# Opening of a two-layer encoder summed on TensorE, the recurrence's output transposed one unit later, and one weight's low part moved

## The reference

```python
mods = (jax.nn.silu(c) @ ada_w[i] + ada_b[i]).reshape(bsz, 9, D_MODEL)
h = _modulate(x, mods, 0)                       # x * (1 + scale) + shift
y = _swiglu(h, ffn_w_in[i, 0], ffn_w_out[i, 0])
x = _layer_norm(ALPHA * x + 0.5 * mods[:, 2, None, :] * y, ...)
...
# mixer of layer 1, per head of 128 channels, chunks of 64 tokens, both directions
state = dcy[..., None] * state + einsum('bhsd,bhsv->bhdv', kd, vc)
o = o_f + o_b
o = o * lax.rsqrt(mean(square(o)) + LN_EPS)
o = o * norm_g * silu(gate);  return o @ w_out
```

## Time and profile before

| | us |
|---|---|
| median of 3 runs | 2140.7 (2138.68 to 2141.26) |
| profiled execution, its own time | 2141.63 |
| span of the profiled execution | 2139.9 |
| TensorE matmuls busy | 2097.4 (98%) |
| VectorE busy | 1199.3 (56%) |
| ScalarE busy | 784.7 (37%) |
| GpSimd busy | 246.0 (11%) |

### The profile page before, as it was taken

How to read it: one execution, slowest core, us unless ns; L and a number is a source line. 1 busy time by engine, 2 the same in 40 slices (tenths; PEclk the granted TensorE clock), 3 DMA queues, 4 the chain that set the end, 5 groups by cost and what they waited for, 6 DMA issues and landing times.

```text
span 2139.9 us, 30931 instructions
## 1 busy us (share of the span) xinstructions
PE 2097.4 (98%) x10775; PEld 1720.5 (80%) x10775; DVE 1199.3 (56%) x1878; ACT 784.7 (37%) x1142; POOL 246.0 (11%) x238
## 2 busy tenths in 40 slices
PE   7999999999999999999999999999999999999997
PEld 5788888878888888888888888877878788888886
DVE  6766665655557666654535533467676555333344
ACT  4321222455434222222532222376666545322222
POOL 0000000432113000001300000151121131000002
PEclk9999999999999999999999999999999999999999
DMA  9766752332325657643335632332222123323322
GB/s 319 216 184 196 219 174 72 88 109 80 106 70 186 188 176 226 195 125 101 89 98 164 179 98 76 101 102 77 70 77 69 40 70 99 91 85 113 95 73 84
DMA packets 405669, 266.34 MB, mean 124 GB/s; under 512 B 9416, under 2 KB 366184, under 8 KB 405608
## 3 DMA queue, kind: packets, MB, share of 16 engines
q1 hardware_dynamic: 405608, 265.57, 41.5%
HBM read 263.37 MB, written 2.19 MB: 124 GB/s over the span
## 4 chain that ended last, share of the span: by engine, by line
PE 92%; ACT 3%; DVE 3%; issue 1%; POOL 1%; DMA 0%; SPq 0%; ACTq 0%; POOLq 0%; DVEq 0%
PE ps L1483 26%; PE ps L1485 26%; PE ps L1484 26%; PE ps L1498 1%; PE ps L1499 1%; PE ps L1523 1%; PE ps L1761 1%; PE ps L1504 1%; PE ps L1682 1%; PE ps L1708 1%; PE ps L1529 1%; PE ps L1693 1%; DVE w_lo L837 1%; PE ps L1779 1%; PE ps L1515 1%
## 5 line engine op out<-in xcount | busy, mean ns | idle before, releaser
L837 DVE TENSOR_TENSOR w_lo<-raw,w_hi 128x1024 fp32r<-128x1024 f32 (+2 forms) x384 | 429.1, 1119 | 699.4 <-ACT w_hi L601 699.2
L601 ACT ACTIVATE w_hi<-raw 128x1024 fp32r<-128x1024 f32 (+2 forms) x384 | 371.6, 969 | 1104.9 <-PE ps L1485 1067.2
L1483 PE MATMUL ps<-h_hi,w_hi 128*128 128x512 f32 x1744 | 686.8, 394 | 3.6 <-DVE g L846 2.2
L1485 PE MATMUL ps<-h_hi,w_lo 128*128 128x512 f32 x1744 | 679.4, 390 | 0.0
L1484 PE MATMUL ps<-h_lo,w_hi 128*128 128x512 f32 x1744 | 678.9, 389 | 0.0
L1483 PEld LDWEIGHTS ps<-h_hi,w_hi 128*128 128x128 f32 x1744 | 327.4, 188 | 79.0 <-issue 8.3
L1485 PEld LDWEIGHTS ps<-h_hi,w_lo 128*128 128x128 f32 x1744 | 327.4, 188 | 68.9
L1484 PEld LDWEIGHTS ps<-h_lo,w_hi 128*128 128x128 f32 x1744 | 327.6, 188 | 65.9
L1483 PE MATMUL ps<-g_hi,w_hi 128*128 128x512 f32 x704 | 276.0, 392 | 0.0
L1485 PE MATMUL ps<-g_hi,w_lo 128*128 128x512 f32 x704 | 274.1, 389 | 0.0
L1484 PE MATMUL ps<-g_lo,w_hi 128*128 128x512 f32 x704 | 274.0, 389 | 0.0
(11 more groups left out here) (252 smaller groups left out, 1943.6 us busy)
## 6 DMA issues: line engine op xcount, KB each, us to landing
raw<-in_ffn_w_in_dram SPq DMA_DIRECT2D x176, 512.0 KB, 3.7
ada_raw<-in_ada_w_dram SPq DMA_DIRECT2D x128, 512.0 KB, 4.3
raw<-in_ffn_w_out_dram SPq DMA_DIRECT2D x64, 384.0 KB, 3.4
raw<-in_ffn_w_out_dram SPq DMA_DIRECT2D x64, 320.0 KB, 3.1
raw<-in_hgrn_w_in_dram SPq DMA_DIRECT2D x40, 512.0 KB, 3.7
raw<-in_na_w_qkv_dram SPq DMA_DIRECT2D x24, 512.0 KB, 3.7
boot<-in_ada_w_dram SPq DMA_DIRECT2D x8, 512.0 KB, 6.8
boot<-in_ada_w_dram SPq DMA_DIRECT2D x16, 256.0 KB, 6.1
```

Source lines behind the costliest of these rows:

```text
L601: nc.scalar.activation(w_hi[s][:, 0:ph.kt, :], raw[s][:, 0:ph.kt, :], ACT.Copy).then_inc(S.w_hi_done, 1)
L837: nc.vector.tensor_tensor(w_lo[s][:, 0:ph.kt, :], raw[s][:, 0:ph.kt, :], w_hi[s][:, 0:ph.kt, :].bitcast(F32), ALU.subtract).then_inc(S.w_l ...
L1483: nc.tensor.matmul(ps[:, bank, :], w_hi[s][:, k, :], a, start=start and k == 0, stop=False)
L1485: ins = nc.tensor.matmul(ps[:, bank, :], w_lo[s][:, k, :], a, start=False, stop=stop and k == ph.kt - 1)
```

## The change

- **Opening.** `boot_steps` and `reduce_boot` go. TensorE now multiplies each row with the matching column of silu(c), broadcast to 32 stationary columns, in four calls of 32 output partitions each (`boot_row`), accumulating over the eight rows in bank 7. VectorE copies the sums (`boot_rows`), TensorE transposes them (`boot_rows_turned`), and `boot_columns` reads them in the row bank. Of the 22 pacing matmuls (12 in `boot_idle`, 10 in `boot_busy`) nine of the short kind are left (3 + 6 in `boot_idle`). The order of the opening changes on TensorE, VectorE, ScalarE and the SP queue. VectorE makes the high parts of the second and third weights. ScalarE runs one small Silu early. In pass 1 of the first phase both engines finish before they convert, and the ride's steps stand behind all four units.
- **Recurrence.** `out_turned(i - 2)` moves behind the second unit, `gated(i - 2)` on VectorE from s = 0 to s = 2, and GpSimd's gate product behind the queries. After the last head `out_turned` and `gated` move in the same sense.
- **Step into the recurrence.** VectorE makes the fourth weight's low part behind the tiles' low parts there. It stays where it was ahead of the feed-forward phases.

```diff
 drive:
                 def steps(i):
+                    opening = ph.n == 0 and isinstance(i, int)
                     for s in range(ph.body):
-                        if ph.kind == "na":
+                        if ph.kind == "na" or opening:
                             finish(ph, i - 1, s)
                             convert(ph, i, s)
                         else:
                             convert(ph, i, s)
                             finish(ph, i - 1, s)
-                        if ride is not None and ph.ada is not None:
+                        if ride is not None and ph.ada is not None and not opening:
                             if s == 2:
                                 gather(ph, i - 1)
+                            ride(ph, i, s)
+                    if ride is not None and opening:
+                        for s in range(ph.body):
                             ride(ph, i, s)
 SP:
-                        sp.wait_ge(S.ada_step, 4)
+                        sp.wait_ge(S.boot_used, 4)
                     elif row == 0:
-                        sp.wait_ge(S.acc_out_ready, 1)
+                        sp.wait_ge(S.ada_reduced, 1)
...
-            for row in range(8):
+            for row in range(4):
                 boot_load(1, row)
             load(phases[0], 0, 2)
+            for row in range(4, 8):
+                boot_load(1, row)
 ScalarE:
+            nc.scalar.activation(warm[:], one[:], ACT.Silu)
             for k in range(4):
                 x_across(k)
             convert(phases[0], 0, 0)
-            convert(phases[0], 0, 1)
             boot_h(0)
             for k in range(4, KT):
                 x_across(k)
-            convert(phases[0], 0, 2)
+            act.wait_ge(S.w_hi_done, 3)
             convert(phases[0], 0, 3)
 VectorE, recurrence:
                 if ph.kind == "hg" and isinstance(i, int) and i == ph.iters - 1:
                     masked(i, 0)
+                    masked(i, 1)
+                    states(i, 0)
                     gated(i - 1)
-                    states(i, 0)
-                    masked(i, 1)
                     states(i, 1)
...
-                if s == 0 and not (isinstance(i, int) and i < 2):
+                if s == 2 and not (isinstance(i, int) and i < 2):
                     gated(i - 2)
 VectorE, opening:
+            def boot_convert_high(s):
+                dve.wait_ge(S.w_loaded[s], lot(phases[0], 0, s))
+                dve.wait_ge(S.w_hi_done, s)
+                nc.vector.tensor_scalar(w_hi[s][:], raw[s][:], 1.0, None, ALU.mult).then_inc(S.w_hi_done, 1)
+
+            def boot_rows(q):
+                at, n = boot_place(q)
+                dve.wait_ge(S.ada_reduced, q + 1)
+                nc.vector.tensor_copy(mod_rows[:, at:at + n], ps[:, BOOT_BANK, at:at + n]).then_inc(S.boot_copied, 1)
...
+            boot_rows(0)
+            boot_columns(0)
+            convert(phases[0], 0, 0)
+            boot_convert_high(1)
+            convert(phases[0], 0, 1)
+            for k in range(0, 4):
+                low_parts(0, k)
+            boot_convert_high(2)
+            convert(phases[0], 0, 2)
+            boot_rows(1)
+            convert(phases[0], 0, 3)
+            boot_columns(1)
+            low_parts(0, 4)
+            low_parts(0, 5)
+            boot_rows(2)
             boot_columns(2)
 VectorE, after a layer norm:
-                if nxt is not None and nxt.body > 3:
+                if nxt is not None and nxt.kind == "in":
                     convert(nxt, 0, 3)
...
                 low_parts(n + 1, KT - 1)
+                if nxt is not None and nxt.kind == "hg":
+                    convert(nxt, 0, 3)
 GpSimd, gates:
                 nc.gpsimd.tensor_tensor(q_raw[:], q_raw[:], q_sig[:], ALU.mult).then_inc(S.qs_done, 1)
-                pool.wait_ge(S.ev_done, i * 5 + 5)
-                if later:
-                    pool.wait_ge(S.n2_done, i)
-                nc.gpsimd.tensor_tensor(gt[:], gt_raw[:], gt_sig[:], ALU.mult).then_inc(S.gs_done, 1)
...
+                pool.wait_ge(S.ev_done, i * 5 + 5)
+                if later:
+                    pool.wait_ge(S.n2_done, i)
+                nc.gpsimd.tensor_tensor(gt[:], gt_raw[:], gt_sig[:], ALU.mult).then_inc(S.gs_done, 1)
 TensorE:
+            def boot_row(q, k):
+                at, n = boot_place(q)
...
+                for c in range(HT):
+                    row = ps[c * ROW_GROUP:(c + 1) * ROW_GROUP, BOOT_BANK, at:at + n].rearrange("p (m c) -> p m c", c=P)
+                    ins = nc.tensor.matmul(row, c_silu[:, k:k + 1].to_broadcast([P, ROW_GROUP]), w[:, :, c * P:(c + 1) * P],
+                                           start=k == 0, stop=k == KT - 1, skip_group_check=True)
+                ins.then_inc(S.ada_reduced if k == KT - 1 else S.boot_used, 1)
...
+            for k in range(0, 4):
+                boot_row(0, k)
+            x_turned(range(0, 4))
+            boot_row(0, 4)
...
+            for k in range(5, KT):
+                boot_row(0, k)
+            boot_idle(3)
+            boot_rows_turned(0)
+            boot_idle(6)
             boot_high(0, range(0, 4))
             boot_high(1, range(0, 4))
+            x_turned(range(4, KT))
+            boot_low(0, range(0, 4))
+            boot_low(1, range(0, 4))
+            for k in range(KT):
+                boot_row(1, k)
             boot_high(2, range(0, 4))
+            boot_rows_turned(1)
+            boot_low(2, range(0, 4))
             pe.wait_ge(S.xt_done, KT)
+            boot_high(3, range(0, 4))
             boot_low(3, range(0, 4))
+            for k in range(KT):
+                boot_row(2, k)
+            boot_high(0, range(4, 6))
+            boot_high(1, range(4, 6))
+            boot_rows_turned(2)
+            boot_high(2, range(4, 6))
+            boot_high(3, range(4, 6))
...
-                            if s == 0 and not (isinstance(i, int) and i < 2):
+                            if s == 1 and not (isinstance(i, int) and i < 2):
                                 out_turned(i - 2)
...
                     hgrn(last, 0)
-                    out_turned(last - 1)
                     out_part(nxt, 1, range(0, 6), (S.ev_done, 5 * ph.iters))
                     hgrn(last, 1)
+                    out_turned(last - 1)
```

More of the change, by code:

```diff
@@ L89 @@
 BOOT_K0 = [0, 4, 6, 8]
-BOOT_DVE = [8, 7, 7]
-BOOT_BASE = [0, 7, 13]
 BOOT_Q = 3
-BOOT_STEPS = 19
+BOOT_BANK = 7
 X_BANK = [4, 5, 3]
@@ L1077, in gated, with ada_steps @@
                                         ALU.subtract).then_inc(S.ho_ready, 1)
-            def ada_steps(slot, steps, k, w, row, last, arrived, width=HM):
+            def ada_steps(ride, steps, k, w, row, last, arrived, width=HM):
                 dve.wait_ge(*arrived)
                 if k == 0:
-                    if not (isinstance(slot, int) and slot == 0):
-                        dve.wait_ge(S.acc_out_ready, slot)
+                    if not (isinstance(ride, int) and ride == 0):
+                        dve.wait_ge(S.acc_out_ready, ride + 1)
                     nc.vector.tensor_scalar(acc[:, 0:width], w, c_silu[:, row:row + 1], None, ALU.mult).then_inc(S.ada_step, 1)
@@ L1091, in ada_steps @@
                     return
-                if not (isinstance(slot, int) and slot == 0):
-                    dve.wait_ge(S.ada_reduced, slot)
+                dve.wait_ge(S.ada_reduced, ride + BOOT_Q)
                 nc.vector.scalar_tensor_tensor(out=acc_out[:, 0:width], in0=w, scalar=c_silu[:, row:row + 1], in1=acc[:, 0:width],
@@ L1099, in ride_ada @@
                 for k in (2 * s, 2 * s + 1):
-                    ada_steps(ride + BOOT_Q, ride * (KT - 1) + BOOT_STEPS, k, ada_raw[s][:, k % 2, :], k, KT - 1,
+                    ada_steps(ride, ride * (KT - 1) + (KT - 1), k, ada_raw[s][:, k % 2, :], k, KT - 1,
                               (S.ada_loaded[s], ride * 16 + 16))
[L1103 to L1110, removed]
+            def boot_convert_high(s):
[6 more added lines that the diff above has]
+                nc.vector.tensor_copy(mod_rows[:, at:at + n], ps[:, BOOT_BANK, at:at + n]).then_inc(S.boot_copied, 1)
             def copy_rows(ph, i):
@@ L1261, in _ @@
             dve.wait_ge(S.silu_c, 1)
-            boot_steps(0, range(8))
             dve.wait_ge(S.vec_mm, 2)
@@ L1601, in x_turned @@
-            def x_turned(h):
-                pe.wait_ge(S.x_loaded[h], 16)
-                for k in range(h * HT, (h + 1) * HT):
+            def boot_row(q, k):
+                at, n = boot_place(q)
+                if q == 0:
+                    w = boot[k][:].rearrange("p (m c) -> p m c", m=2)
+                    pe.wait_ge(S.boot_loaded[k], 16)
+                else:
+                    b = (q - 1) * 4 + k // 2
+                    w = boot[b][:, (k % 2) * HM:(k % 2 + 1) * HM].rearrange("p (m c) -> p m c", m=1)
+                    pe.wait_ge(S.boot_loaded[b], 48)
+                for c in range(HT):
[3 more added lines that the diff above has]
```

(18 more changed lines are left out.)

64 lines of the change are left out of this document (14 added, 50 removed).

## The result

The changed kernel took 2144.91 us (median of 20 runs, 2142.24 to 2149.22), the kernel before beside it 2141.74 (2138.68 to 2144.06): a ratio of 1.0016, 95% interval 1.0011 to 1.0022. That is slower by 3.2 us between the medians: inside the prediction's middle case (within 0.2% of the kernel before), and outside its range of 2127.5 to 2140. The profiled execution took 2146.35 for a span of 2144.6; the one before took 2141.63 for 2139.9. The spans differ by 4.7.

The account below looks back on a forecast made before the run. TensorE, busy 98% of the span, was taken as the bound. Opening -6.0, step -1.6, loop +3.2 and tail -0.5 sum to -4.9: from the median 2140.7 to 2135.8 us, range 2127.5 to 2140.

Parts of the forecast that it names:

- middle case: Whole kernel: time within 0.2% (4.3 us) of the kernel before, chance 0.3.
- Opening, forecast -6.0: Kernel's start: TensorE sums the boot rows, loop of units starts at about 52.1 instead of 58.40; -6.0 us.
- rival 5: Opening: column groups do not overlap, a row sum costs 1.13 us instead of 0.35; slower, 2148; chance 0.05.
- the first product: Opening: TensorE's first real product was put at 22.2, against 24.34 before.
- The ride's wait: Opening: the ride's steps end at about 63.3 on VectorE, TensorE asks at 63.0; 0.3 us charged.
- Rival 4: Opening gives less: slow TensorE pace or late group 1 rows, -1 to -3; 2138 to 2140; chance 0.08.
- Step into the recurrence, forecast -1.6: Before the recurrence: moving the fourth weight's low part removes TensorE's 1.31 wait for h_hi and a refill; -1.6 us.
- the 1.4 us wait on the q gate stays: Step into the recurrence: TensorE's q gate wait hangs on products that move with it, so stays at 1.4 us.
- Loop, forecast +0.54 a pass: Recurrence: transpose wait goes, 1.06 gained, but moved gate makes states late, 1.6 wait; six passes, +3.2 us.
- rival 3: Recurrence loop: GpSimd's back-to-back products hold L1076, states 0.35 later a pass, 2.1 us in all; 2137.9; chance 0.12.
- rival 2: Recurrence loop: L1074 starts ahead of GpSimd, gate takes 1.9 to 2.9, loop -6.4 to -1.6; 2126 to 2131; chance 0.3.
- Tail, forecast -0.5: Last head: old waits of 2.1 us go, but TensorE waits 1.6 at L1770 for am_both; -0.5 us.

Follow-up runs that it names:

- e6: Kernel before with only the new opening (row sums on TensorE in column groups, ride behind the body): 2135.61 us, ratio 0.9975 to the kernel before.
- e2: Kernel before with only the recurrence's order changed (output's transpose, gate and GpSimd's gate product moved): 2148.74 us, ratio 1.0032 to the kernel before.
- e7: e5 with the fourth weight's low part back at its old place: 2128.66 us, ratio 0.9935 to the kernel before.
- e11: e7 run once more, unchanged: 2126.44 us, ratio 0.9923 to the kernel before.
- e5: Changed kernel with GpSimd's sum ahead of its gate product (released by the high part) and VectorE's last two gate operations behind the states: 2127.81 us, ratio 0.9936.
- e8: Changed kernel with VectorE's last two gate operations behind the states, GpSimd's order left as it was: 2136.93 us, ratio 0.9975 to the kernel before.
- e3: Changed kernel with the fourth weight's low part back at its old place, ahead of the fifth tile's scaling: 2142.99 us, ratio 1.0004 to the kernel before.

## Why the prediction was wrong, step by step

**Opening, forecast -6.0: right.** The units start 6.7 earlier and stand 5.9 ahead at L1658; e6 gives -0.25%, -5.4 us (-7.7 to -3.2). A row sum took 0.24 instead of 0.35, so rival 5 is out (0.66 was its point); the first product came 0.7 later than put. The ride's wait is 0.86 where 0.3 was charged. Rival 4 is out too: the loop starts well ahead of 56. (Its own sum would be 2138.8 to 2140.8, and not 2138 to 2140.) By the profile, 1.5 of the gain was given back at the first layer norm, where L1544's two groups took 1.94 and 1.71 us instead of 1.14 and 1.08, at a clock of 0.90 in the window. That stretch is not the opening's: e2 has it with the old opening, and of e7 and e11, one and the same kernel, the first lacks it and the second has it (1.89 and 1.77). It differs between executions, and how many of the timed runs had it is not known.

**Step into the recurrence, forecast -1.6: right; "the 1.4 us wait on the q gate stays": this sentence failed.** The move alone gave -1.66 at the first head and +3.97 in the pass behind it. The wait was taken to hang on TensorE's products, and it hangs on GpSimd: three low parts in a row beside four scalings stretch these from 6.4 to 8.5, and that is passed on by the constants, the scan, the exponentials and the table load to the gate: 1.9 to 2.5 us. The rest of the 3.97, 1.5, lies at the lower clock behind the longer wait. The step moved an operation past VectorE's queue and did not ask who runs beside it in its new place.

**Loop, forecast +0.54 a pass: right in mechanism, mis-sized.** Measured +0.94 in the table, 0.96 in one pass. The gain was 1.26 instead of 1.06 (from the pass's first L1769 to L1790 TensorE takes 21.05, and took 22.31). The gate took 4.08 instead of 3.73 in four of the six passes, exactly the 0.35 of rival 3. In the other two rival 2's condition came true, L1085 at 0.43 and the gate at 3.0, and its saving did not: the scan was held instead. The prediction took the hold for a property of L1085 and L1087; it falls on what VectorE starts while GpSimd's two products run, and they run for 2.7 us in one piece. As the pass up to there had become 0.2 shorter, the states end only 0.13 later than forecast: 25.52 after the pass's first L1769 (1540.19 - 1514.67), against 25.39. And L1737 starts 0.42 behind the last state instead of the 0.12 charged for the last product: another 0.3 a pass. The Trainium skill (SBUF — State Buffer, Who interferes with whom) says that copies and tensor_scalar in their two-port modes, and operations with two SBUF inputs, contend with GpSimd, and that issue order decides who blocks. The traces agree, though they do not show which mode an operation ran in: L1085, a tensor_scalar, took 1.56 beside GpSimd and 0.42 in e5, L1036 1.60 against 0.69, and in e8 the scan came first and the gate product was stretched.

**Tail, forecast -0.5: wrong sign.** By the table, this part of the profile became 1.45 longer. The wait at L1790 is 2.3, not 1.6: GpSimd's products took 1.44 and 1.71 there beside VectorE's gate instead of 1.29 and 1.49. The turn alone costs 0.3 behind the last head (e2, 450.9 against 450.6). In the changed kernel and in e3 the same wait was followed by a stretch at half the clock (0.94 in the window), and there this part is 1.4 longer than before; in e2 it was not.

In sum: the loop's six passes cost 2.4 more than forecast, the pass behind the q gate 3.5, the first norm 1.5 and the tail 1.9. With -4.9 that makes +4.4 of the +4.7 in the profile; the medians' +3.2 cannot be split in this way. Rival 3 as worded gives 2137.9: its mechanism is shown, but most of the miss lies outside it, in the q gate, which stood in no case.

## What to carry to other kernels

A piece of VectorE's work can be moved to a unit where TensorE no longer waits for it and still lose, if it lands ahead of a chain that TensorE needs in the same pass: move only the operation that frees the bank, and put the rest behind the chain. Where GpSimd is released by the operation that is moved, look at what VectorE does in the microseconds after it; here the order of two GpSimd products was worth 6.5 us between the medians (2144.91 against 2138.37, each beside the kernel before at 2141.7). And a wait that the profile shows before a change is not fixed: follow its chain back over all engines before writing that it stays.

## What the runs showed of the hardware

- A seven-column VectorE operation (L1047) took 1.25 us beside a GpSimd sum and 0.16 without (e8, e5): a small operation is held as well.
- A scan that starts before GpSimd's product runs at its own pace (1.21) and the product takes 2.07 instead of 1.29 (e8); one that starts while GpSimd's sum runs is held: 2.31 at 1496.36 in the changed kernel.
- A TensorE wait of 3.4 to 3.9 us for the q gate cost its own length and 1.3 to 1.6 us more at the lower clock; waits of 1.4 to 2.6 us did not, in the same place. For the 2.3 us wait of the last head it fell out both ways.
- A boot row, four column-group calls of 128 columns in fp32, took 0.24 us (eight in 1.95).
